# Grouped-query attention with keys on the partitions and the maxima from a pass ahead

## The reference

```python
def attend(q, k, v):
    qg = q.reshape(B, Lq, kvh, H // kvh, hd)
    s = jnp.einsum('bqkgd,bskd->bkgqs', qg, k).astype(jnp.float32) * ATTN_SCALE
    p = jax.nn.softmax(s, axis=-1).astype(v.dtype)
    o = jnp.einsum('bkgqs,bskd->bqkgd', p, v)
```

## Time and profile before

| | us |
|---|---|
| median of 3 runs | 1341.53 (1341.21 to 1342.74) |
| the profiled execution, its own time | 1341.3 |
| its span, first to last instruction | 1339.4 |
| TensorE busy | 1304.5 (97%) |
| VectorE busy | 961.8 (72%) |
| ScalarE busy | 670.5 (50%) |
| GpSimd busy | 200.0 (15%) |

### The profile page before, as it was taken

How to read it: one execution, slowest core, us unless ns; L and a number is a source line. 1 busy time by engine, 2 the same in 40 slices (tenths; PEclk the granted TensorE clock), 3 DMA queues, 4 the chain that set the end, 5 groups by cost and what they waited for, 6 DMA issues and landing times. The chain is left out here.

```text
span 1339.4 us, 23131 instructions
## 1 busy us (share of the span) xinstructions
PE 1304.5 (97%) x8096; PEld 719.7 (54%) x8096; DVE 961.8 (72%) x1573; ACT 670.5 (50%) x1288; POOL 200.0 (15%) x140
## 2 busy tenths in 40 slices
PE   7999999999898999999999999999999999999997
PEld 1564666445676777777445444444444444444443
DVE  4779886676788999997345986666666666566387
ACT  2532134434897888887314554455444445312225
POOL 0000000221009400000001233222223330000001
PEclk9999999999999999999999999999999999999999
DMA  9637611051513003000013032222222213997953
GB/s 373 224 125 283 248 32 63 1 172 50 190 49 127 0 31 94 0 0 2 33 62 94 1 87 87 86 86 86 78 78 78 66 51 115 311 342 262 352 193 130
DMA packets 106704, 158.85 MB, mean 119 GB/s; under 512 B 8208, under 2 KB 67088, under 8 KB 104848
## 3 DMA queue, kind: packets, MB, share of 16 engines
q1 hardware_dynamic: 106640, 158.00, 34.5%
HBM read 135.95 MB, written 19.93 MB: 116 GB/s over the span
## 5 line engine op out<-in xcount | busy, mean ns | idle before, releaser
L980 PE MATMUL PS<-arena 128*128 128x512 f16 (+6 forms) x6856 | 1188.0, 332 | 14.3 <-DMA arena<-in_w_mod 6.8
L980 PEld LDWEIGHTS PS<-arena 128*128 128x128 f16 (+3 forms) x6856 | 601.0, 102 | 548.0 <-issue 37.3
L2436 DVE SCALAR_TENSOR_TENSOR arena<-arena 128x512 f16<-128x512 f32 x148 | 119.9, 817 | 76.7 <-ACT arena L1797 76.7
L1797 ACT ACTIVATE arena<-arena 128x512 f16<-128x512 f32 x140 | 87.6, 629 | 130.4 <-PE PS L980 130.4
L2368 DVE SCALAR_TENSOR_TENSOR arena<-PS,arena 128x512 f16<-128x512 f32 (+2 forms) x256 | 131.4, 565 | 3.0 <-ACT arena L1735 3.0
L1735 ACT ACTIVATE arena<-PS 128x512 f16<-128x512 f32 (+2 forms) x256 | 111.3, 503 | 33.0 <-PE PS L1292 33.0
L1292 PE MATMUL PS<-arena 128*128 128x128 f32 x800 | 113.9, 280 | 7.4 <-DMA arena<-arena 1.9
L1725 ACT ACTIVATE arena<-PS,arena 128x1280 f32<-128x1280 f32 (+1 forms) x96 | 111.2, 1158 | 5.5 <-DVE arena L2360 2.6
L1909 ACT ACTIVATE arena<-arena 128x512 f16<-128x512 f32 x77 | 48.2, 629 | 128.7 <-DVE arena L2584 75.7
L2360 DVE TENSOR_REDUCE arena<-PS 128x1 f32<-128x1280 f32 x64 | 95.5, 1492 | 23.0 <-PE PS L980 23.0
L1292 PEld LDWEIGHTS PS<-arena 128*128 128x128 f32 x800 | 85.3, 141 | 39.2 <-ACT arena L1725 25.5
(11 more groups left out here) (177 smaller groups left out, 977.1 us busy)
## 6 DMA issues: line engine op xcount, KB each, us to landing
arena<-in_w_ffn_out SPq DMA_DIRECT2D x121, 256.0 KB, 4.7
arena<-in_w_mod SPq DMA_DIRECT2D x24, 1024.0 KB, 7.3
arena<-in_w_ffn_in SPq DMA_DIRECT2D x88, 256.0 KB, 3.0
arena<-in_w_in SPq DMA_DIRECT2D x9, 1024.0 KB, 5.8
left_operands<-arena SPq DMA_DIRECT2D x33, 256.0 KB, 2.2
arena<-left_operands SPq DMA_DIRECT2D x3, 2816.0 KB, 15.0
arena<-lay_bias SPq DMA_DIRECT2D x4, 1536.0 KB, 9.1
arena<-in_x SPq DMA_DIRECT2D x2, 2048.0 KB, 14.0
```

What stands on the lines that cost most here:

```text
L980: return pe.matmul(out, lhsT, rhs, start=start, stop=stop, skip_group_check=True)
L1797: act.activation(aS[n % RING][:, 0], weight_block(p, b), ACT.Copy, scale=WS).then_inc(blk_hi, 1)
L2436: dve.scalar_tensor_tensor(dst[:, 1], src, WS, dst[:, 0], ALU.mult, ALU.subtract).then_inc(blk_lo, 1)
```

## The change

The grouped-query attention is laid out the other way. A step (`Step`) is one tile of 128 keys against four heads side by side, 4 x 128 queries, so 512 columns; ten steps are a group (one key head, one query tile), and sixteen groups, 160 steps, are the stage. Per step:

- TensorE makes the scores with the keys on the partitions: two matmuls of 512 columns (`step_scores`), into one of three PSUM banks. The second adds the low part of the keys and, through rows that hold ones, the negative maximum of each query, so that the scores come out shifted.
- ScalarE takes the exponential twice, once into float16 (`Pt`, five buffers) and once into float32 (`Pf`, four buffers).
- The low part is their difference, read from SBUF twice: on VectorE for six of ten tiles (`step_low`), on GpSimd for the tiles 1, 4, 6 and 8 (`low_p2`).
- TensorE multiplies with the values with the probabilities as weights: eight matmuls (`step_weigh`), four of 129 columns for the high part and four of 65 for the low part, four steps behind the scores. The values have a column of ones, which gives the row sums.

The maxima come from a pass ahead, thirteen steps early: one more score product with the high part of the keys alone, 512 columns per step (`chunk`), of which VectorE takes the maximum (`chunk_maximum`). Once per group VectorE builds the shifts from them (`query_shifts`), TensorE turns them (`turn_shifts`), ScalarE copies them (`copy_shifts`), and GpSimd copies the high part of the queries (`high_queries`). At a group's end ScalarE copies the outputs (`copy_outputs`), VectorE inverts the sums, and GpSimd adds and scales (`group_output`).

The splitting of the output weights on GpSimd is cut into sixteen parts of 512 columns (`part_of_out`): three before the first group, then one in each of the first thirteen groups. Of the residual rows, the last quarter is loaded only after the last step. The values of the grouped-query heads move to a tensor of their own.

```diff
+LEAD, LAG, SHIFT_AT, SEND_AT = 13, 4, 8, 4
+RING_P, RING_F = 5, 4
+POOL_TILES = (1, 4, 6, 8)
+CHUNK_BANK, STEP_BANK, SHIFT_BANK = (5, 0), (1, 2, 4), 3
...
+            def part_of_out(i):
...
+                own.step(pool.tensor_scalar(r, r, WS / HS if n < 2 and k < 2 else WS, None, ALU.mult))
                 own.wait()
-                own.step(pool.tensor_copy(woS[n][:, 0], r))
+                own.step(pool.tensor_copy(dst[:, 0, k], r))
                 own.wait()
...
+                ins = pool.tensor_tensor(dst[:, 1, k], r, dst[:, 0, k], ALU.subtract)
...
+            def low_p2(n):
...
+                pool.tensor_tensor(pt[:, 1], Pf[n % RING_F], pt[:, 0], ALU.subtract).then_inc(pt_lo2, 1)
...
+            for g in range(NGROUP):
+                if g < 13:
+                    part_of_out(3 + g)
+                if g + 1 < NGROUP:
+                    high_queries(g + 1)
+                for i in POOL_TILES:
+                    low_p2(NKT * g + i)
+                    if i == SEND_AT and g:
+                        group_output(g - 1)
+            group_output(NGROUP - 1)
...
+            def step_scores(s):
...
+                mm(PS[:, s.bank], kT[:, s.kv, 0, keys], heads(s), True, False)
...
+                mm(PS[:, s.bank], kT[:, s.kv, 1, keys], q2[s.kv], False, True).then_inc(st_mm, 1)
...
+            def step_weigh(s):
...
+                    for part, a in ((0, 0), (1, HD)):
+                        ins = mm(PS[:, 6 + h // 2, o + a:o + 2 * HD + 1], pt[:, part, h * P:h * P + P],
+                                 v[:, a:2 * HD + 1], s.i == 0 and h % 2 == 0 and part == 0, s.i == NKT - 1 and part == 1)
...
+            def step(s):
+                step_scores(s)
+                for c in s.chunks():
+                    chunk(c)
+                if s.i == SHIFT_AT and s.s + NKT < NSTEPS:
+                    turn_shifts(s.ahead(NKT - SHIFT_AT))
+                if s.s >= LAG:
+                    step_weigh(s.ahead(-LAG))
...
+            def step_probabilities(s):
...
+                act.activation(Pt[s.s % RING_P][:, 0], PS[:, s.bank], ACT.Exp).then_inc(pt_hi, 1)
...
+                act.activation(Pf[s.s % RING_F], PS[:, s.bank], ACT.Exp).then_inc(s_exp, 1)
...
+            def chunk_maximum(c):
...
+                dve.tensor_reduce(out, ps, AX, ALU.max).then_inc(s_max, 1)
...
+            def step_low(s):
+                if s.by_pool:
+                    return
+                dve.wait_ge(pt_hi, 2 * NNA + s.n + 1)
+                dve.wait_ge(s_exp, NNA + s.n + 1)
+                pt = Pt[s.s % RING_P]
+                dve.tensor_tensor(pt[:, 1], Pf[s.s % RING_F], pt[:, 0], ALU.subtract).then_inc(pt_lo, 1)
```

More of the change, by code:

```diff
@@ L238, with __init__ @@
 class Unit:
[L242 to L251, removed]
+    def __init__(self, v):
+        self.v, self.par, self.blk, self.j = v, v % 2, v // 8, v % 8
+        self.banks = [range(0, 3), range(3, 5)]
@@ new lines, in _ @@
+            pool.wait_ge(pr_tc, NU)
+            own.step(pool.memset(shifts, 0.0))
+            own.wait()
+            high_queries(0)
+            pool.wait_ge(s_mm, NNA)
+            for i in range(3):
+                part_of_out(i)
+            for g in range(NGROUP):
[7 more added lines that the diff above has]
+                        group_output(g - 1)
@@ new lines, in scores @@
+                q, k = nqT[:, u.blk, u.j * P:u.j * P + P], nkT[:, u.blk]
+                half, col = u.j // 4, KEY_COL[u.j % 4]
+                if bias_kind(u.j) % 2:
+                    pieces = (("ctx", 0, 0, 256), ("near", 256, 0, 8), ("near", 512, 8, 12))
+                else:
+                    pieces = (("near", 0, 0, 12), ("ctx", 384, 0, 128), ("ctx", 512, 128, 256))
+                for what, o, a, b in pieces:
+                    ps = PSf[:, 1536 * u.par + o:1536 * u.par + o + (b - a) * (K_COLS if what == "near" else 1)]
+                    for part in range(2):
+                        if what == "near":
+                            ps = ps.rearrange("p (r c) -> p r c", c=K_COLS) if part == 0 else ps
+                            keys = k[:, part, 0:S].rearrange("p (r c) -> p r c", c=GRID_W)
+                            keys = keys[:, 4 * half + a:4 * half + b, col:col + K_COLS]
+                        else:
+                            keys = k[:, part, S + a:S + b]
+                        ins = mm(ps, q, keys, part == 0 and o in (0, 512), part == 1)
@@ new lines, in weigh @@
+                copied(u, 1)
+                for i in range(5):
+                    m = i - 2 * (bias_kind(u.j) % 2)
+                    if 0 <= m < 3:
+                        v = nearV[u.j % 4][:, u.j // 4 + m, u.blk]
+                    else:
+                        v = V[:, NT + m % 3, u.blk] if m > 0 else V[:, NT + m + 2, u.blk]
+                    for part, vp in ((0, 0), (1, 0), (0, 1)):
+                        ins = mm(PS[:, 6 + u.par, 0:HD], PT[:, u.par, part, i], v[:, vp],
+                                 i == 0 and part + vp == 0, i == 4 and vp == 1)
@@ L1370, in turn_mix @@
                 ins.then_inc(mx_mm, 1)
[L1372 to L1377 removed]
+            for i in range(3):
+                turn_mix(i)
+                step_weigh(Step(NSTEPS - LAG + i))
+            step_weigh(Step(NSTEPS - 1))
             turn_mix(3)
@@ new lines, in copy_outputs, with step @@
+            def copy_outputs(s):
+                if s.s >= 2 * NKT:
+                    act.wait_ge(oab_sum, s.g - 1)
+                act.wait_ge(o_mm, NNA + s.n + NKT)
+                for b in range(2):
+                    act.copy(oraw[s.kv][:, 2 * b:2 * b + 2].rearrange("p h d -> p (h d)"),
+                             PS[:, 6 + b, 0:4 * HD + 2]).then_inc(o_rdy, 1)
+            def step(s):
+                if s.i == SEND_AT and s.s >= NKT:
+                    copy_outputs(s.ahead(-NKT - SEND_AT))
+                step_probabilities(s)
+                if s.i == SHIFT_AT and s.s + NKT < NSTEPS:
+                    copy_shifts(s.ahead(NKT - SHIFT_AT))
```

447 lines of the change are left out of this document (284 added, 163 removed).

## The result

The changed kernel takes 1347.66 us (median of 8 runs, 1344.1 to 1351.14) against 1341.89 us (8 runs, 1341.21 to 1343.59) for the kernel before. The ratio is 1.004, 95% interval 1.0025 to 1.0054: slower by 0.4%, where 0.8% faster was forecast and the range ended at 1347. The profiled execution took 1347.17 us, its span 1345.4.

The account below looks back on a forecast made before the run. TensorE bound the old kernel; VectorE and GpSimd, holding each other, would set 12.8 us a group. The stage sums to 201.4 us, ending at 619.6 against 630.9; 11.3 gained less 0.5 gives 1331 us, range 1303 to 1347.

Parts of the forecast that it names:

- The start of the stage: Grouped-query attention: first exponential near 413.4 us, after the last unit's work, nine maxima, shifts, turn, copy and second product.
- GpSimd's unseen sizes: GpSimd at 512 columns, mostly without rows: scaling 1.47 us, cast 0.6, subtraction and low part 1.2, copy at most 0.6.
- VectorE's low parts: Six per group on VectorE: 0.60 us each plus 0.34 net waiting for GpSimd, both inputs being in SBUF.
- ScalarE's sum: ScalarE per group: twenty exponentials, one copy of 512 columns and two of 258, 10.8 us.
- The squares: VectorE's mean wait: GpSimd instruction lengths squared over twice the period; squares sum to 11.2, giving 0.44 us, 0.34 net.
- GpSimd's side: GpSimd per group: 10.4 us of work plus six holds of 0.41 us, 12.9 us.
- The shifts, three tiny dependent instructions: VectorE's building of the shifts, once per group: put at 0.6 us.
- VectorE's sum: VectorE per group: maxima 6.1, low parts 3.6, shifts 0.6, inverse sums 0.15, 10.45 us; with waits 12.5.
- rival 2: GpSimd's block before tile 1 holds in-order TensorE, ScalarE runs dry: 14.4 us a group, 1352 us; chance 0.18.
- a lower clock: TensorE's clock might drop; argued against by 349 to 360 us, busy 8.65 of 11 us at clock 1.00.
- Rival 1: VectorE's waits hide in GpSimd's gaps and ScalarE sets the pace: 10.9 us a group, about 1305 us; chance 0.22.
- Rival 3: Stage shortens but a late load delays projection or first feed-forward block; lower clock acts likewise: 1341 us; chance 0.06.

Follow-up runs that it names:

- e10: The changed kernel run once more, unedited: 1347.5 us, ratio 1.0039 to the kernel before.
- e6: Changed kernel with low parts' second operand from PSUM (low parts left out), negated maxima in PSUM, and weight parts cut to one column (projection left out): 1313.7 us.
- e5: Changed kernel with VectorE's six low parts taking their second operand from the PSUM bank of the maxima's scores, low parts thereby left out: 1323.1 us, ratio 0.9864.
- e2: Changed kernel with each group's negated maxima (128x4) kept in the shifts' PSUM bank instead of SBUF, same arithmetic: 1333.2 us, ratio 0.9945.
- e4: Changed kernel with the pass ahead for the maxima leading by fourteen steps instead of thirteen: 1341.2 us, ratio 1.0007.
- e7: Changed kernel with negated maxima in PSUM and the lead of fourteen steps together, same arithmetic: 1339.4 us, ratio 0.9986.
- e11: Changed kernel with negated maxima in PSUM and GpSimd's copy of the next queries moved between tiles 6 and 8: 1343.2 us, ratio 1.0026.
- e9: Changed kernel with negated maxima in PSUM and the float32 exponentials of tiles 0, 3 and 5 in the shifts' PSUM bank: 1325.7 us, ratio 0.988.
- e12: Kernel with negated maxima and three exponentials in PSUM, plus GpSimd's query copy moved between tiles 6 and 8: 1319.3 us, ratio 0.9837.
- e1: Changed kernel with the float32 exponential of VectorE's six tiles written back into its PSUM bank, TensorE waiting before reusing it: 1361.3 us, ratio 1.015.
- e3: Changed kernel with GpSimd's sixteen output-weight parts working on one column instead of 512, projection result left out: 1330.5 us, ratio 0.994.

## Why the prediction was wrong

**What held.** The start of the stage was put at 413.4 and came at 413.45; that is closer than it deserves, since the terms written down add up to 413.1, and the same kernel run again (e10) started at 415.1. GpSimd's unseen sizes came within a tenth: scaling 1.49 (1.47 forecast), cast 0.61 (0.6), subtraction and low part 1.16 (1.2), copy 0.60, each unhindered. VectorE's low parts were to cost 0.60 + 0.34, and did 0.95 (mean length 1.03 less the 0.08 by which neighbours overlap). ScalarE's sum, 10.8, shows in e6 as 11.2 busy in a group of 11.33. The mechanism, VectorE's low parts held by GpSimd, is shown by e5: with one operand in PSUM all 87 take 0.67 to 0.69 us and the time falls by 1.8%. The Trainium skill, "SBUF — State Buffer", section "SBUF: two separate sides", puts it as whoever starts first holding the pair for its whole instruction; this case agrees for two-input GpSimd work (VectorE ends 0.55 us behind it), but not for the one-input scaling: a low part that met its first 0.13 us was released some 0.6 us into it (1.02 us, in the changed kernel), and one that met its last 0.23 was not held (0.68 us, in e2).

That the mean hold came out as forecast, 0.35 for 0.34, is in part luck. The squares count the scaling with its whole length, and they take the meetings as random, while the traces repeat the same meetings group after group. GpSimd's side was put too high: the holds add about 1.6 us a group to its instructions and not six times 0.41, it is busy for 11.2 us a group where 12.9 was summed, and it still waits 17.1 of 130 us for exponentials.

**The step that failed.** "The shifts, three tiny dependent instructions, I put at 0.6." They read and write four columns, and I priced them by their size. But the two that add the bound work from SBUF to SBUF and are held like the low parts, the first of them almost always, although it reads only one tensor besides the per-partition bound: 0.17, 0.94 and 0.31 us in the mean, with the gaps 1.5 us a group. VectorE's sum is then 6.1 + 5.7 + 1.5 + 0.15 = 13.45, and 13.54 is the middle group. e2 takes only this away and lands at 12.86 us a group, where 12.8 was forecast, and at 1333 us, where 1331 was. The term is 0.9 us a group too small. It makes VectorE's 12.5 to 13.4 and so accounts for the middle of the stage, 7.9 of the 16.7 us by which the profiled execution missed; the rest lies at the end of the stage and behind it. That e2 meets the forecast so closely has some luck in it, because the low parts kept their mean there: in e4 and e7 the shifts are free too, and low parts of 1.10 us leave 13.31 and 13.27 us a group.

**The end of the stage.** Thirteen groups took 176.1 us, 7.9 over the 168.2 forecast with its three extra maxima, and the last three 38.4 to the end of the last exponential, 5.2 over. There the shifts cost more than their length:

```profile
611.60 1.09 DVE L2609 TENSOR_SCALAR arena<-arena 128x4 f16<-128x4 f32 x1
612.72 1.07 DVE L2611 SCALAR_TENSOR_TENSOR arena<-arena 128x4 f16<-128x4 f32 x1
...
614.50 0.58 ACT L1920 CAST arena<-PS 64x512 f16<-64x512 f32 x1 [2.03 <-PE PS L1086]
616.00 0.60 ACT L1927 ACTIVATE arena<-PS 128x512 f16<-128x512 f32 x1 [0.93 <-PE PS L1086]
```

Both are held, one after the other, so the shifts are ready only at 613.8; TensorE stands in order before them, ScalarE idles 2.0 and then 0.9 us. This is rival 2's mechanism, TensorE held in order, but behind VectorE's shifts and not behind GpSimd's tile 1: TensorE waited 0.3 us in 130 for L1009. The clock adds to it:

```profile
609.00:612.00 3.00, 2.18 (x24) 1.20 (x22) 2.93 (x6) 3.00 (x7) 2.76 (x4) 1.00 0.00 0
612.00:615.00 3.00, 1.15 (x13) 1.15 (x14) 2.95 (x4) 0.97 (x2) 1.76 (x2) 0.81 0.00 0
615.00:618.00 3.00, 3.00 (x24) 1.72 (x23) 0.69 (x1) 1.68 (x5) 0.00 (x0) 0.62 0.02 5
```

TensorE, busy for 1.15 of 3 us while it waits, then works through 615 to 618 us mostly at the lower level of 1.2 GHz (0.62). In e2 the same groups take 11.9 and 11.7 us instead of 13.0 and 14.9, and the clock is 1.00 throughout; how much of the difference is the hold and how much the clock that followed it, no run separates.

**After the stage.** The projection's first twelve matmuls ran in part at half the clock:

```profile
633.29 4.28 PE L1086 MATMUL PS<-arena 128*128 128x512 f16 x12 [2.40 <-DVE arena L2701]
```

4.28 us for what took 2.75. The granted clock was 1.00 from 633 to 634 us and 0.57 from 634 to 638, so most of the twelve ran at the lower level of 1.2 GHz. From 627 to 633 us, before the projection, TensorE had been busy for 2.96 of 6 us. Before the change it was busy for 18.7 of the 20 us from 620 to 640, at 1.00. I had ruled a lower clock out by one window of 79% busy at full clock; that row was not enough. It costs 1.5 us. It does not follow each time: in e4 TensorE was busy for 1.37 of the 3 us from 627 to 630 and the clock stayed at 1.00 to 633. The projection started 2.4 us later than before instead of 11.3 earlier, and the feed-forward part 4.1 later; the profiled execution then lost another 1.9 us behind its loads of the last weights and at its end, which is not explained further.

**The rivals.** Rival 1 is what e6 came near, at 1313.7 for 1305, once the holds were gone. Rival 2's pace from 13.65 on is close to what was measured (13.54 and, in e10, 13.70), but not for its reason, as said above. Rival 3 wanted a shorter stage and a late load; the stage itself ended 2.4 us later, though the lower clock that it names did come and cost 1.5 us.

**Still open.** Why one edit moves the holds up and another down. e4, e7 and e11 each change when a low part meets GpSimd, and the mean went to 1.10, 1.10 and 1.13, in e9 and e12 to 0.93 and 0.86, with three of six freed. A random meeting is a fair mean for a first estimate and no forecast for a given order. What lets GpSimd's next instruction go ahead of the waiting VectorE is known only in part: behind the copy it does so whenever it is ready; behind an addition or subtraction VectorE goes first nearly always, also before a scaling (in e2, e4, e7, e9 and e12), but in ten groups of e11 the scaling goes first.

## What to carry to other kernels

Where VectorE and GpSimd both work from SBUF, list for each VectorE instruction its kind and how many of its tensors lie in SBUF, the four-column ones too: a held instruction costs what GpSimd is doing, not what it does itself. Moving one operand to PSUM freed each kind that was tried here. It pays if it does not keep a bank from TensorE: e1 put the exponentials into banks that TensorE needed and lost, e9 put three of them into a spare one and gained. Measure again after each edit, because the holds that are left move: e4 freed the shifts and lengthened the low parts. With two engines nearly full, take the sum as a floor and expect the order of their work to be worth a percent either way.

## What the runs showed of the hardware

- A VectorE subtraction with two SBUF tensors ends 0.54 to 0.55 us after the end of the GpSimd addition, subtraction or copy that held it, against 0.68 alone.
- A GpSimd scaling of 128x512 (1.49 us) did not hold it to its end: begun 0.13 us behind the scaling, the VectorE subtraction took 1.02 us; begun 0.23 us before its end, 0.68.
- An addition of 128x4 with one SBUF tensor and a per-partition scalar, SBUF to SBUF, was held too (up to 1.09 us beside a GpSimd subtraction, 3.59 beside a GpSimd MEMSET in e3). A maximum from SBUF to SBUF was not: 0.17 us, sixteen of sixteen in the changed kernel, and within the same fill in e3. So the number of SBUF tensors alone does not tell; which property of the addition does was not tried.
- With the tensor in PSUM and a per-partition scalar in SBUF, the addition was not held; nor was the subtraction with a PSUM tensor, such a scalar and one SBUF tensor (0.23 us, sixteen of sixteen, in e2). So the scalar did not count as a second operand there.
- A VectorE instruction can be held through two GpSimd instructions: 2.11 us when a low part started straight behind a copy (39 of 39), 1.59 us when a scaling followed a low part (ten groups of e11).
- Idle time of TensorE in a busy stage can be paid for by the next stage: busy for 2.96 of 6 us ahead of the projection, TensorE then ran it at a granted clock of 0.57 from 634 to 638 us.
